# Group A's keys, the first block's loads and the fills, moved ahead of the end of the input projection

## The reference, cut to what matters

```python
proj = jnp.einsum('bld,dc->blc', x, w_in)            # 2048 tokens, 1024 -> 2560 + 196 columns
qa, ka, va, ga, qi, ki, wi, qb, kb, vb, gb = jnp.split(proj, offsets, axis=-1)
# group A: per block of 128 queries
dots  = jnp.einsum('bqhd,bsd->bqhs', qi_blk, ki)     # indexer, 4 heads
score = jnp.einsum('bqh,bqhs->bqs', w_blk * idx_scale, jax.nn.relu(dots))
_, idx = lax.top_k(score, 256)                       # among the visible keys
p = jax.nn.softmax(q_blk . k_sel * 64**-0.5 - slopes * |t - idx|)
out_a = p . v_sel                                    # 8 heads, one shared key/value head
# group B: window of 128 keys, 8 heads, 2 key/value heads, ALiBi and a learned sink in the softmax
y = jnp.concatenate([ya * silu(ga), yb * silu(gb)], axis=-1)
x = layer_norm(alpha * x + y @ w_out)
```

## Time and profile before

| | us |
|---|---|
| median of 3 runs (range) | 1454.12 (1453.76 to 1454.82) |
| the profiled execution, its own time | 1462.23 |
| its span, first to last instruction | 1460.4 |
| PE, DVE, ACT, POOL busy in the span | 1359.3, 1130.6, 896.8, 629.6 |
| mean granted TensorE clock | 0.964 of full speed |

### The profile page before, as it was taken

The page is one execution under the profiler, slowest core; times in us unless marked ns, Lnnn a source line. Parts: engine busy times, 40 slices in busy tenths (PEclk is TensorE's granted clock), DMA queues, the critical chain, the costliest instruction groups (busy, mean ns, idle before and its releaser), DMA issues. The chain is left out here.

```text
span 1460.4 us, 18810 instructions
## 1 busy us (share of the span) xinstructions
PE 1359.3 (93%) x6006; PEld 993.5 (68%) x6052; DVE 1130.6 (77%) x2215; ACT 896.8 (61%) x1687; POOL 629.6 (43%) x726
## 2 busy tenths in 40 slices
PE   7999999899999995798999799999999799999997
PEld 5888887698888874565655456655555565588886
DVE  3486879864899887778889999889898967257675
ACT  3395885873498736777775488885678676700010
POOL 2421332633422336466544256534336577423332
PEclk9999999999999996699999999999999899999999
DMA  7412232325232328233433132402011143134442
GB/s 241 127 60 80 87 105 80 117 91 154 73 109 94 101 90 174 66 89 87 113 92 88 45 83 56 104 21 64 27 28 26 39 133 118 44 122 146 144 148 83
DMA packets 106548, 136.85 MB, mean 94 GB/s; under 512 B 6643, under 2 KB 83383, under 8 KB 106191
## 3 DMA queue, kind: packets, MB, share of 16 engines
q1 hardware_dynamic: 93296, 93.23, 23.4%
q10 hardware_dynamic: 9504, 31.66, 5.5%
q0 software_dynamic: 3648, 10.76, 2.5%
HBM read 92.20 MB, written 42.34 MB: 92 GB/s over the span
## 5 line engine op out<-in xcount | busy, mean ns | idle before, releaser
L1644 DVE TENSOR_SCALAR_CACHE_REDUCE above<-dist,trial 128x512 bf16<-128x512 int32 (+13 forms) x224 | 345.9, 1544 | 28.9 <-POOL trial L1002 23.9
L1179 ACT ACTIVATE above<-dist,trial 128x384 bf16<-128x384 int32 (+13 forms) x224 | 280.8, 1254 | 60.8 <-DVE trial L1617 24.3
L1356 PE MATMUL psum<-x_hi,w_hi 128*128 128x512 f32 x640 | 251.8, 393 | 16.0 <-DVE x_lo L1693 10.6
L1356 PE MATMUL psum<-x_lo,w_hi 128*128 128x512 f32 x640 | 250.8, 392 | 0.0
L1356 PE MATMUL psum<-x_hi,w_lo 128*128 128x512 f32 x640 | 250.5, 391 | 0.0
L1290 ACT ACTIVATE prob<-psum 128x512 f32<-128x512 f32 x272 | 159.8, 593 | 115.8 <-PE psum L1506 54.6
L1748 DVE CUSTOM_DVE_ANT_0 junk<-psum,mask 128x512 bf16<-128x512 f32 (+3 forms) x320 | 184.4, 605 | 26.7 <-PE psum L1430 16.1
L1506 PE MATMUL psum<-prob,vw 128*65 128x512 f32 x376 | 184.8, 597 | 0.1
L1493 PE MATMUL psum<-qa_mix,ka_mix 128*128 128x512 f32 x272 | 162.4, 597 | 5.5 <-DMA qa_ext<-minus_max 3.7
L1430 PE MATMUL psum<-ka_ext,qa_ext 128*128 128x512 f32 (+3 forms) x320 | 134.1, 467 | 27.4 <-ACT ka_mix L1129 12.3
L941 POOL CAST w_hi<-raw 128x1024 fp32r<-128x1024 f32 x40 | 49.7, 1243 | 253.1 <-PE psum L1356 248.8
(11 more groups left out here) (161 smaller groups left out, 2906.8 us busy)
## 6 DMA issues: line engine op xcount, KB each, us to landing
raw<-w_tiles SPq DMA_DIRECT2D x40, 512.0 KB, 3.7
proj<-staged ACTq DMA_DIRECT2D x40, 512.0 KB, 3.3
qb_raw<-proj SPq DMA_DIRECT2D x32, 256.0 KB, 4.0
qa_raw<-proj SPq DMA_DIRECT2D x32, 256.0 KB, 4.5
yt_raw<-y_t SPq DMA_DIRECT2D x16, 512.0 KB, 5.1
x_row<-x_res SPq DMA_DIRECT2D x16, 512.0 KB, 3.9
out<-z ACTq DMA_DIRECT2D x16, 512.0 KB, 2.6
x_raw<-xT SPq DMA_DIRECT2D x12, 512.0 KB, 4.2
```

What stands on the lines that cost most here:

```text
L1179: nc.scalar.activation(above[:, 0, 0:n], src, ACT.Sign, scale=-1.0, bias=u, accum_out=count[:, 0:1]).then_inc(sign_counted, 1)
L1356: last = pe.matmul(psum[:, 2 * u + m, :], wt[:, u, k, :], xt[:, k, 512 * m:512 * m + 512], start=(k == 0 and q == 0), stop=(k == KT - 1 an ...
L1644: v.tensor_scalar(above[:, 1, 0:n], src, u, None, ALU.is_ge, ALU.add, accum_out=count[:, 1:2]).then_inc(own_counted, 1)
```

## The change

Group A's keys load into the buffers of `values_hi` and `values_lo` in four DMAs, right after their tile is stored; the waits between them and `relu` go, and `split_values` waits for the keys' copies in place of the other way round. `last_tile(k)` is a wait for step k of the last weight tile's eight; `x_used` is raised at these steps for the second half too. With it `load_qa` of block 0 waits for step 0, `load_bias` for step 1, `extra_rows` for step 4, `shift_values` for step 5 and `round_qa` for step 6. The six fills of DVE and that of `row_top` become `fill` on POOL: six after steps 2 and 5, the last after step 7. `scan` of block 0 waits for 39 tiles moved out of PSUM in place of 40. `qa_raw` moves to the start of the late buffers, and `junk` and `y_a` ahead of `yt_a` and `gate_a`. Every number of `PREFER` is another (not shown), so the order is planned anew; the plan counts `decide_own` and `decide_sign` at 0.53 us in place of 0.45, `load_keys_a` at 1.4 and `shift_values` at 3.6. All other waits on `setup_dve` become waits on `filled` at 6, `setup_pool` at 3 becomes 2.

```diff
+FILLS = 7
...
-                add("POOL", 0.45, "decide_own", p, i, needs=[("search", p, i)])
+                add("POOL", 0.53, "decide_own", p, i, needs=[("search", p, i)])
...
-    add("SP", 0.7, "load_keys_a", needs=[sums[-1], ("store", 1, 2)])
+    last = lambda k: ("product", 1, N_TILES - 1, k)
+    add("SP", 1.4, "load_keys_a", needs=[("store", 1, 2)])
     for i in range(2):
-        add("ACT", 3.2, "round_keys_a", i, needs=[("load_keys_a",), ("keys_rest", 1), ("norm", NORM_ORDER[-1])])
+        add("ACT", 3.2, "round_keys_a", i, needs=[("load_keys_a",), ("split_x2", 2 * KT + 1), ("norm", NORM_ORDER[-1])])
         add("POOL", 2.6, "split_keys_a", i, needs=[("round_keys_a", i)])
     add("POOL", 1.0, "load_power", needs=[("split_w", 1, N_TILES - 1)])
-    add("SP", 0.4, "load_bias", needs=[end])
-    add("POOL", 3.2, "extra_rows", needs=[end])
+    add("SP", 0.4, "load_bias", needs=[last(1)])
+    add("POOL", 3.2, "extra_rows", needs=[last(4), ("load_power",)])
     add("ACT", 1.0, "setup_act", needs=[end])
-    add("DVE", 1.8, "setup_dve", needs=[end])
-
-    add("ACT", 0.25, "put_sink", 0, needs=[("setup_dve",)])
-    add("SP", 0.8, "shift_values", needs=[end, ("leave_norm", NORM_ORDER[-1])])
+    for i in range(2):
+        add("POOL", 0.35 if i else 2.2, "fill", i, needs=[end if i else last(5), ("fill", i - 1)])
+
+    add("ACT", 0.25, "put_sink", 0, needs=[("fill", 0)])
+    add("SP", 3.6, "shift_values", needs=[last(5), ("leave_norm", NORM_ORDER[-1])])
 
...
-        add("SP", 0.7, "load_qa", b, needs=[("split_qa", b - 1)] + ([end] if first else []))
+        add("SP", 0.7, "load_qa", b, needs=[("split_qa", b - 1)] + ([last(0), ("store", 1, 7)] if first else []))
...
-        add("ACT", 1.75, "round_qa", b, needs=[("load_qa", b)] + ([last_values(b - 2)] if b >= 2 else [end]))
+        add("ACT", 1.75, "round_qa", b, needs=[("load_qa", b)] + ([last_values(b - 2)] if b >= 2 else [last(KT - 2)]))
...
-                       ("extra_rows",), ("load_power",), ("round_keys_a", 1), ("evacuate", 1, N_TILES - 1)])
+                       ("extra_rows",), ("load_power",), ("round_keys_a", 1), ("evacuate", 1, N_TILES - 2)])
             scan_list.append(("scan_max", *scan))
-            add("DVE", 0.16 + w * 0.00104, "scan_max", *scan, needs=[("scan", *scan), ("load_mask", b), ("setup_dve",), scan_list[-2], *stores])
+            add("DVE", 0.16 + w * 0.00104, "scan_max", *scan, needs=[("scan", *scan), ("load_mask", b), ("fill", 1), scan_list[-2], stores[1], end])
...
-                add("POOL", 1.4 + 1.3 * i, "split_values", i, needs=[("leave_norm", NORM_ORDER[-1]), ("split_values", i - 1)])
+                add("POOL", 1.4 + 1.3 * i, "split_values", i, needs=[("leave_norm", NORM_ORDER[-1]), ("split_keys_a", 1), ("split_values", i - 1)])
...
-        keys_a_raw = flat(relu)
+        keys_a_raw = [values_hi[:, :, :].bitcast(F32).rearrange("p b n -> p (b n)")[:, 0:HALF],
+                      values_lo[:, :, :].bitcast(F32).rearrange("p b n -> p (b n)")]
+
+        def last_tile(k):
+
+            return (x_used, KT + k) if k < KT - 1 else (tile_mm, 2 * N_TILES)
+
...
-                    sp.wait_ge(tile_mm, 2 * N_TILES)
+                    sp.wait_ge(*last_tile(0))
...
-                sp.wait_ge(summed, 4 * chunks_before(NPAIR - 2))
-                for r in range(2):
-                    sp.dma_start(keys_a_raw[HD * r:HD * r + HD, :], proj[ROW_KA:ROW_KA + HD, :]).then_inc(keys_in, 16)
+                for i in range(2):
+                    for r in range(2):
+                        sp.dma_start(keys_a_raw[i][HD * r:HD * r + HD, :],
+                                     proj[ROW_KA:ROW_KA + HD, HALF * i:HALF * i + HALF]).then_inc(keys_in, 16)
...
-                sp.wait_ge(tile_mm, 2 * N_TILES)
+                sp.wait_ge(*last_tile(1))
                 sp.dma_start(bias[:, :, :], c_bias).then_inc(bias_in, 16)
 
             def shift_values():
-                sp.wait_ge(tile_mm, 2 * N_TILES)
+                sp.wait_ge(*last_tile(5))
                 sp.wait_ge(norm_out, NB)
                 sp.dma_start(vs[0:HD, 1:NB, :], vw[HD:P, 0:NB - 1, HD + 1:HD + 1 + P]).then_inc(values_shifted, 16)
...
-                nc.gpsimd.tensor_tensor(ka_mix[0:HD, ks], keys_a_raw[0:HD, ks], ka_ext[0:HD, 0, ks].bitcast(F32),
+                nc.gpsimd.tensor_tensor(ka_mix[0:HD, ks], keys_a_raw[i][0:HD, :], ka_ext[0:HD, 0, ks].bitcast(F32),
...
-                pool.wait_ge(tile_mm, 2 * N_TILES)
+                pool.wait_ge(*last_tile(4))
                 for i in range(2):
                     pool.dma_start(qa_ext[HD:P, i, :, :], c_extm.bitcast(F32R)).then_inc(late_in, 16)
                 pool.dma_start(upper[:, :, :], c_upper.bitcast(F32R)).then_inc(late_in, 16)
-                settled()
-                nc.gpsimd.memset(row_top[:, :], 0.0).then_inc(setup_pool, 1)
-                latest[0] = (setup_pool, 2)
+
+            def fill(top):
+
+                pieces = [(2, mask[:, 0, 0:P], 0.0), (2, mask[:, 1, 0:2 * P], 0.0), (2, mask[0:HD, 0, HD:P], -BIG),
+                          (2, mask[0:HD, 1, P + HD:2 * P], -BIG), (2, lb[:, :, 0:HD], 0.0), (5, vs[0:HD, 0, :], 0.0),
+                          (KT - 1, row_top[:, :], 0.0)]
+                for i in ((FILLS - 1,) if top else range(FILLS - 1)):
+                    k, where, value = pieces[i]
+                    pool.wait_ge(*last_tile(k))
+                    settled()
+                    nc.gpsimd.memset(where, value).then_inc(filled, 1)
+                    latest[0] = (filled, i + 1)
 
             def decide_own(p, i):
                 steps = 32 * (p - 1) + i + 1
...
+                    pool.wait_ge(keys_taken, 2)
...
-                if n_dots == 2 * chunks_before(NPAIR - 2):
-                    act.wait_ge(keys_lo, 2)
...
-                act.wait_ge(keys_in, 32)
+                act.wait_ge(keys_in, 64)
+                act.wait_ge(x_lo_ok, 2 * KT + 2)
                 act.wait_ge(norm_mm, NB)
-                copy(ka_ext[0:HD, 0, ks], keys_a_raw[0:HD, ks]).then_inc(keys_hi, 1)
-                copy(ka_ext[0:HD, 1, ks], keys_a_raw[0:HD, ks])
-                copy(ka_mix[HD:P, ks], keys_a_raw[HD:P, ks]).then_inc(keys_taken, 1)
+                copy(ka_ext[0:HD, 0, ks], keys_a_raw[i][0:HD, :]).then_inc(keys_hi, 1)
+                copy(ka_ext[0:HD, 1, ks], keys_a_raw[i][0:HD, :])
+                copy(ka_mix[HD:P, ks], keys_a_raw[i][HD:P, :]).then_inc(keys_taken, 1)
...
-                    act.wait_ge(tile_mm, 2 * N_TILES)
+                    act.wait_ge(*last_tile(KT - 2))
...
-                    act.wait_ge(setup_dve, 1)
+                    act.wait_ge(filled, FILLS - 1)
...
-                elif (half, t) == (0, N_TILES - 1):
+                elif t == N_TILES - 1:
...
-                    pe.wait_ge(tile_out, 2 * N_TILES)
+                    pe.wait_ge(tile_out, 2 * N_TILES - 1)
...
-                    pe.wait_ge(setup_pool, 2)
+                    pe.wait_ge(filled, FILLS)
...
-            def setup_pieces():
-                dve.wait_ge(tile_mm, 2 * N_TILES)
-                dve.wait_ge(const_in, 16)
-                v.memset(mask[:, 0, 0:P], 0.0)
-                step(v.memset(mask[:, 1, 0:2 * P], 0.0))
-                v.memset(mask[0:HD, 0, HD:P], -BIG)
-                step(v.memset(mask[0:HD, 1, P + HD:2 * P], -BIG))
-
-                v.memset(vs[0:HD, 0, :], 0.0)
-                v.memset(lb[:, :, 0:HD], 0.0).then_inc(setup_dve, 1)
...
-                    for i in range(2):
-                        dve.wait_ge(stored[i], 16 * N_TILES)
+                    dve.wait_ge(stored[0], 16 * N_TILES)
+                    dve.wait_ge(tile_mm, 2 * N_TILES)
+                    dve.wait_ge(filled, FILLS)
```

More of the change, by code:

```diff
@@ L348, in whole_plan @@
             add("DVE", 1.45, "bias_b", b, g,
[L349 removed]
+                needs=[("window", b, g), ("turn_b", b - 1), ("load_bias",), ("fill", 0), ("put_sink", b), ("exp_b", b - 1, H - 1)])
         for h in range(H):
@@ L368, in whole_plan @@
         add("SP", 0.4, "place_max", b, needs=[("leave_max", b), ("positions", b)])
-        add("PE", 0.9, "turn_b", b, holds="banks2", until=("copy_b", b), needs=[("level_b", b), ("setup_dve",), ("mix_b", b - 1)])
+        add("PE", 0.9, "turn_b", b, holds="banks2", until=("copy_b", b), needs=[("level_b", b), ("fill", 0), ("mix_b", b - 1)])
         add("ACT", 1.03, "copy_b", b, needs=[("turn_b", b), ("mix_b", b - 1)])
```

25 lines of the change are left out of this document (12 added, 13 removed).

## The result

The changed kernel took 1470.29 us (1469.17 to 1474.29), the kernel before 1453.94 beside it: ratio 1.0118, interval 1.0096 to 1.0139. It is slower by 17 us by this ratio, 16 by the medians, where I had forecast 7 us less.

The account below looks back on a forecast made before the run. PE, busy 93% of the span, loses time at the projection-attention seam through idling and low clock. From the 1454.1 us median, 7.0 us for an earlier first `scan_max`, other terms 0, gave 1447.1 us; range 1439 to 1454.

Parts of the forecast that it names:

- Keys: Projection: ACT's copies (6.1 us), POOL's two splits and 1 MB of loads move there; cost 0, without cover at most 6.1 us.
- queries: Seam: block 0's queries load after step 0, their copies come after step 6, by about 557, never last; cost 0.
- extra rows: Seam: issued from 551.3, landing 5.1 to 10.9 us after issue, so the first scan could start between 560.0 and 565.8.
- fills: Seam: DVE loses 1.2 us; POOL's six take 1.2 to 5.6, taken as 2.5; cost 0, at the upper end 1 to 2.
- the stall that I had weighed: Landing of `upper`: up to 2.03 of its 10.9 us may be DMA descriptors stalled by DVE's two-port mode, absent after the change.
- "larger" rival: Seam: `bias_b` and scans go ahead of sortable, rows land in about 5 us; 1442, or 1439 with clock; chance 0.21.
- From the first `scan_max` to `place_max` [...] the chain is 7.6 us as now: Seam, block 0: this chain keeps its 7.6 us, and the first logits come 2.6 us after the issue of `place_max`.
- The term of 7.0 us: Seam: with DVE deciding, the first `scan_max` comes at 567.4 instead of 574.36, 7.0 us earlier, counted to the end.
- given back: Behind the seam: DVE's masks come no earlier, the block at 820 waits as before; 1452 to 1454; with nothing happening 0.17.
- Does it last?: After the seam: DVE's whole stream, search included, moves equally, so the 7.0 us hold to the end: 1447.1 us.
- no mean, and up to 4 us either way: Replanned order of all the rest, which no row prices: given no mean, up to 4 us either way in the range.
- slower: Seam: rows land late, DVE stands at block 0's `scan_max` with sortable queued behind, stream 5.7 us later; 1460; chance 0.10.

Follow-up runs that it names:

- second trace of before: The kernel before, unchanged, traced again with the experiments: span 1451.8 us, 8.6 less than the first trace; median 1453.62 us (one).
- s_new_r_old: Changed code with its own order up to block 0's `place_max`, then the order of the kernel before: 1454.14 us, ratio to before 0.9992 (0.9982 to 1.0001).

## Why the prediction was wrong

**Keys, queries, extra rows, fills: right.** No cost of them shows in the projection (PE is busy 532.8 us up to 556, 531.1 in the second trace of before). `extra_rows` was issued at 546.6, earlier than the 551.3 I had worked out, since POOL's split ended at 546.6 in the new order, and `upper` took 6.0 us: near my lower end. How much of the 4.9 us less than before is the stall that I had weighed, and how much the emptier DMA engines (share 0.68 in the 28 us from 556, where the second trace has 0.99), no run tells. The fills took 2.1 us against my 2.5.

**DVE's order: the "larger" rival's.** `bias_b` and the scans went ahead of sortable, and `turn_max` was 16 us early. It didn't reach the end.

**First failed step: "From the first `scan_max` to `place_max` [...] the chain is 7.6 us as now".** It took 19.5 us (558.5 to 578.0), and from that issue to the first logits 5.0 us where I had 2.6. I had gone through SP's queue for what stands behind block 0's load, not for what stands ahead of `place_max`. Sortable now stood between `turn_max` and `leave_max`, and two waiting loads ahead of `place_max`. The term of 7.0 us measured 1.2 in `s_new_r_old`. Mending both queues brought the logits to 571 and only 1.7 us more. The likely reason is that the search of p = 5 on DVE, ACT and POOL sets the pace from there; that was my rival "given back", with the search as its place and not the masks near 820. It also answers "Does it last?".

**Second failed step: the rest of the order, "no mean, and up to 4 us either way".** It measured 23.6 us with the old seam, 18.3 with the new one (1.0118 less 0.9992), joins included. My range held no such case, and my *slower* rival was of another kind. The evidence was at hand: every weight in `PREFER` had changed, PE and DVE were both nearly full for 205 us, and a wait of 2 us there costs clock besides. What I had no row for I should have given tens of us, not four. The weights alone, on an unchanged list of pieces, were never swapped; what is shown is that the order as a whole lost the time, not which of the new weights or piece costs did.

**Profile and runs.** I took the first trace's 8.1 us over the median across as a constant. It was one stretch of that execution, right behind the seam, and it made the seam of the change look better than it was. I also read the 3.66 us of L1607 against the 2.03 of L1609 as two speeds of DVE; the last section shows a wait in it. And the clock's row had a second, smaller dent, from 1132 to 1168 us, that I passed over; 5 us of the loss come near it.

What stays open: which pieces of the new order lose the 8 us from 900 to 940 us. The rows show 2.9 us of idle PE from 920 to 940 (before has none, and 0.6 more lie from 900 to 920), and 20 us at a clock of 0.74, which I estimate at 5.2 us (0.26 of 20): together they are the step. The longest single wait, and the stretch behind it:

```profile
922.28 0.30 PE L1424 MATMUL psum<-kb_hi,qb_mix 128*128 128x128 f32 x1 [1.70 <-DVE yt_b L1786]
924.00:932.00 8.00, 6.77 (x25) 4.65 (x25) 7.59 (x28) 6.85 (x24) 5.84 (x9) 0.50 0.47 143
```

No run took one of these waits away.

## What to carry over

When an order is planned anew, an edit at one seam changes the places of pieces everywhere: swap in half of the old order before you believe that the edit and not the replanning moved the time. When a step comes early, follow it through the queue of every engine up to its last reader, here a copy on DVE and a DMA on SP; a 15 us piece on a nearly full engine holds someone wherever it stands. Take two traces of the kernel before, and compare the gain of a stretch with what differs between them. A long wait is not the measure of what a place costs: count the work on both sides, and weigh it.

## What I had not expected of the hardware

POOL's splits beside DVE's sortable took 2.62 us (128x384) and 7.81 us (two of 64x512), as shown above. In the second trace of before the same, with DVE at block 0's short `scan_max` and idle between them:

```profile
576.95 1.00 POOL L1020 TENSOR_TENSOR kb_lo<-kb_raw,kb_hi 128x384 fp32r<-128x384 f32 x1
578.03 2.50 POOL L1024 TENSOR_TENSOR qb_mix<-qb_raw,qb_mix 64x512 fp32r<-64x512 f32 x2
```

The slow pair began while DVE ran L1627, with two tensors read from SBUF, and ended 1.1 us after L1628 had. The Trainium skill, SBUF — State Buffer, section "SBUF: two separate sides", calls this a lock on a pair of ports that is held for a whole instruction; these rows agree with it. The same happened the other way round in the kernel before, whose first step of sortable took 3.66 us from 555.82 and the changed kernel's 2.03. Ahead of it stood, in the first trace:

```profile
555.18 2.42 POOL L964 TENSOR_TENSOR qi_split<-qi_raw,qi_split 64x1024 fp32r<-64x1024 f32 x1 [3.94 <-ACT qi_split L1129]
```

POOL ended at 557.60, and 2.03 us on from there is 559.63, where DVE's step ended at 559.48. These times fit a DVE that waits for POOL's split, with the wait booked as its own duration; an order that puts the two side by side then pays on either engine.

PE's clock moved more time than I had thought: 6.6 of the 17.7 us. And it doesn't need a long wait: near 922 us PE had idled 1.70 us, and the granted clock was 0.76 from 922 to 924, 0.50 from 924 to 932 and 1.00 from 934 on. Behind the 11.1 us wait, the same kind of matmul on either side of it, at the level of 2.4 GHz (granted 1.00 from 1160 to 1168) and then at that of 1.2 (0.50 from 1181 to 1185):

```profile
1168.11 0.40 PE L1532 MATMUL psum<-prob_hi,values_lo 128*64 128x512 f32 x1
1179.60 0.69 PE L1534 MATMUL psum<-prob_lo,values_hi 128*65 128x512 f32 x1 [11.09 <-DVE prob_lo L1802]
1180.09 0.63 PE L1531 MATMUL psum<-prob_hi,values_hi 128*65 128x512 f32 x1
1180.51 0.63 PE L1532 MATMUL psum<-prob_hi,values_lo 128*64 128x512 f32 x1
```
